# Two passes in place of three in the up projection of a transformer block, with the halves of a PSUM bank summed at eviction

## The reference

```python
h = rms_norm_2(x, g_pre_ffn) * (1.0 + sc2) + sh2          # 256 x 2048
u = causal_dwconv(h @ w_up, conv_w, conv_b)               # w_up 2048 x 11264, 3 taps over time
y = (silu(u[..., :D_FF]) * u[..., D_FF:]) @ w_down        # D_FF = 5632
x = x + gt2 * rms_norm_2(y, g_post_ffn)

def causal_dwconv(u, w, b):                               # per channel
    y = b
    for j in range(3): y = y + w[j] * up[:, j:j + S]      # up: u padded with 2 zero rows ahead
```

## Time and profile before

| | |
|---|---|
| runs | 2039.69, 2040.11 and 2041.86 us; median 2040.11 us |
| profiled execution | span 2036.7 us from its first to its last instruction; no other time of it is given |
| TensorE | busy 1953.7 us, 96% of the span |
| VectorE, ScalarE | busy 1321.1 us (65%) and 1018.2 us (50%) |
| DMA | 444.82 MB, mean 218 GB/s |
| mean granted TensorE clock | 0.984 |
| up projection | about 1263 to 1774 us of the span; down projection 1781 to 2021 us |

### The profile page before, as it was taken

One profiled execution on the slowest core, in us unless ns is written; L12 is line 12 of the kernel. 1 busy time (PEld: TensorE's weight loads), 2 busy tenths in 40 slices (PEclk: granted clock), 3 DMA queues, 4 the chain that ended last, 5 costly groups with the idle time before them and its releaser, 6 DMA issues.

```text
span 2036.7 us, 33083 instructions
## 1 busy us (share of the span) xinstructions
PE 1953.7 (96%) x11146; PEld 1695.5 (83%) x11146; DVE 1321.1 (65%) x1733; ACT 1018.2 (50%) x1587; POOL 112.6 (6%) x184
## 2 busy tenths in 40 slices
PE   6999999999999999998899998999999999999997
PEld 5888887778788887787778777999999999888885
DVE  5677775675777645557767777666677665655455
ACT  5544545553455454446654444555555555544443
POOL 1000001000000013320000000000000000000001
PEclk9999999998999999999999998999999999999998
DMA  7787786676787763346568885676767765555553
GB/s 255 258 299 251 251 270 198 207 263 238 259 293 256 275 181 115 113 131 219 177 211 280 297 264 177 204 231 225 234 221 230 231 200 183 165 176 192 198 187 124
DMA packets 236153, 444.82 MB, mean 218 GB/s; under 512 B 14125, under 2 KB 109962, under 8 KB 234682
## 3 DMA queue, kind: packets, MB, share of 16 engines
q1 hardware_dynamic: 234666, 434.39, 64.8%
q0 software_dynamic: 1424, 9.63, 1.2%
HBM read 439.72 MB, written 4.24 MB: 218 GB/s over the span
## 4 chain that ended last, share of the span: by engine, by line
PE 83%; DVE 6%; ACT 4%; issue 3%; DMA 3%; SPq 1%; DVEq 0%; ACTq 0%
PE PS L1575 74%; DMA ada_raw<-in_w_ada 3%; ACT w_hi L623 1%; PE PS L1606 1%; PE PS L1657 1%; DVE arena L1050 1%; DVE w_lo L1000 1%; PE PS L1634 1%; PE PS L1660 1%; PE PS L1643 1%; PE PS L1668 1%; DVE s_sb L1158 1%; DVE smx L1166 0%; PE PS L1678 0%; PE PS L1679 0%
## 5 line engine op out<-in xcount | busy, mean ns | idle before, releaser
L1000 DVE TENSOR_TENSOR w_lo<-raw,w_hi 128x1024 fp32r<-128x1024 f32 x618 | 755.7, 1224 | 556.4 <-ACT w_hi L623 549.0
L623 ACT ACTIVATE w_hi<-raw 128x1024 fp32r<-128x1024 f32 x618 | 653.1, 1059 | 734.7 <-PE PS L1575 689.9
L1575 PE MATMUL PS<-w_hi,aT_hi 128*128 128x512 f32 (+1 forms) x1632 | 651.9, 399 | 17.9 <-ACT arena L759 7.3
L1575 PE MATMUL PS<-w_hi,aT_lo 128*128 128x512 f32 (+1 forms) x1632 | 635.9, 390 | 0.0
L1575 PE MATMUL PS<-w_lo,aT_hi 128*128 128x512 f32 (+1 forms) x1632 | 635.1, 389 | 0.0
L1575 PE MATMUL PS<-aT_hi,w_hi 128*128 128x256 f32 x1408 | 398.9, 283 | 0.5 <-DVE aT_lo L1121 0.5
L1575 PE MATMUL PS<-aT_hi,w_lo 128*128 128x256 f32 x1408 | 398.4, 283 | 0.0
L1575 PE MATMUL PS<-aT_lo,w_hi 128*128 128x256 f32 x1408 | 398.4, 283 | 0.0
L1575 PEld LDWEIGHTS PS<-w_hi,aT_hi 128*128 128x128 f32 x1632 | 307.9, 189 | 95.6 <-issue 16.0
L1575 PEld LDWEIGHTS PS<-w_hi,aT_lo 128*128 128x128 f32 x1632 | 307.5, 188 | 64.6
L1575 PEld LDWEIGHTS PS<-w_lo,aT_hi 128*128 128x128 f32 x1632 | 308.2, 189 | 58.8 <-issue 0.2
(11 more groups left out here) (211 smaller groups left out, 1381.9 us busy)
## 6 DMA issues: line engine op xcount, KB each, us to landing
raw<-in_w_in SPq DMA_DIRECT2D x256, 512.0 KB, 4.0
ada_raw<-in_w_ada SPq DMA_DIRECT2D x192, 512.0 KB, 4.9
raw<-in_w_up SPq DMA_DIRECT2D x176, 512.0 KB, 3.5
raw<-in_w_down SPq DMA_DIRECT2D x88, 512.0 KB, 3.9
raw<-in_w_out SPq DMA_DIRECT2D x32, 512.0 KB, 4.8
raw<-in_w_o SPq DMA_DIRECT2D x32, 512.0 KB, 5.6
raw<-in_w_uq SPq DMA_DIRECT2D x18, 512.0 KB, 5.6
raw<-in_w_ukv SPq DMA_DIRECT2D x16, 512.0 KB, 4.0
```

Source lines behind the costliest of these rows:

```text
L623: nc.scalar.activation(w_hi[:, m % RING, :], raw[:, m % RING, :], ACT.Copy).then_inc(hi_ready, 1)
L1000: nc.vector.tensor_tensor(w_lo[:, m % RING, :], raw[:, m % RING, :], w_hi[:, m % RING, :].bitcast(F32), ALU.subtract).then_inc(lo_ready, 1)
L1575: mm = pe.matmul(dst, l, r, start=first and j == 0, stop=last and j == 2)
```

## The change

Activations: `aT_hi` and `aT_lo` become the two halves of one tensor `aT` [128, 16, 2, 256], so that for each k tile [a_hi | a_lo] are 512 contiguous columns. In the up projection a triple of passes becomes two: w_hi over the 512 columns [a_hi | a_lo] into a whole bank, and w_lo over a_hi (256 columns) into its first half. The bank then holds u in two parts. For each of the two tiles of a pair ScalarE copies the second half to SBUF (`cross`, in slots 0 and 1, semaphore `conv_b`), VectorE adds the first half to it in place (`sums`, in slots 1 and 2, semaphore `conv_sum`), and all taps read this sum from SBUF. The buffers of the sums (`halves`) lie in `bias`, which is not otherwise used in this phase. ScalarE's taps move to slots 2 and 3 and its silus to 4 and 5; VectorE's taps move to 3 and 4, its products to 5 and 6, its second GT2 piece to slot 7. The banks are handed back to TensorE by `conv_sum` in place of `conv_d`.

```diff
-        aT_hi = sb("aT_hi", [P, KT, SEQ], F32R)
-        aT_lo = sb("aT_lo", [P, KT, SEQ], F32R)
+        aT = sb("aT", [P, KT, 2, SEQ], F32R)
+        aT_hi, aT_lo = aT[:, :, 0, :], aT[:, :, 1, :]
+        halves = [[bias[:, 2 * SEQ * b + SEQ * k:2 * SEQ * b + SEQ * (k + 1)] for k in range(2)] for b in range(2)]
 # ScalarE, columns_hi (VectorE's columns_lo in the same way)
-                    last = nc.scalar.activation(dst[:, 2 * j:2 * j + 2, :].rearrange("p k t -> p (k t)"), bank,
+                    last = nc.scalar.activation(dst[:, 2 * j:2 * j + 2, :], bank.rearrange("p (k t) -> p k t", k=2),
 # ScalarE, up projection
-            def taps(pair, b, bank):
+            def cross(b, bank):
                 if b == 0:
                     act.wait_ge(chunk_used, T.ready(chunk_used, SLOTS))
+                for k in range(2):
+                    last = nc.scalar.activation(halves[b][k], PS[:, bank + 2 * k, SEQ:2 * SEQ], ACT.Copy)
+                last.then_inc(conv_b, 1)
+
+            def taps(pair, b):
+                act.wait_ge(conv_sum, T.ready(conv_sum))
                 act.wait_ge(y_done, T.free(y_done))
                 for k, (dst, tile) in enumerate(((conv_g[b], pair), (conv_u[b], pair + FT))):
-                    last = nc.scalar.activation(dst, PS[:, bank + 2 * k, 0:SEQ], ACT.Identity,
+                    last = nc.scalar.activation(dst, halves[b][k], ACT.Identity,
...
                 for slot in range(SLOTS):
                     split()
+                    if slot in (2, 3):
+                        taps(before + slot - 2, slot - 2)
                     if slot < 2:
-                        taps(before + slot, slot, (0 if odd else B_UP1) + slot)
-                    if slot in (3, 4):
-                        silu(slot - 3)
+                        cross(slot, (0 if odd else B_UP1) + slot)
+                    if slot in (4, 5):
+                        silu(slot - 4)
...
             up_panel(40, True)
             for b in range(2):
-                taps(42 + b, b, B_UP1 + b)
+                cross(b, B_UP1 + b)
+            for b in range(2):
+                taps(42 + b, b)
 # VectorE, up projection
+            def sums(b, bank):
+                dve.wait_ge(conv_b, T.ready(conv_b))
+                for k in range(2):
+                    last = nc.vector.tensor_tensor(halves[b][k], PS[:, bank + 2 * k, 0:SEQ], halves[b][k], ALU.add)
+                last.then_inc(conv_sum, 1)
+
-            def taps(pair, b, bank):
+            def taps(pair, b):
...
-                            out=dst[:, shift:SEQ], in0=PS[:, bank + 2 * k, 0:SEQ - shift],
+                            out=dst[:, shift:SEQ], in0=halves[b][k][:, 0:SEQ - shift],
...
                     if slot in (1, 2):
-                        taps(before + (slot - 1), slot - 1, (0 if odd else B_UP1) + slot - 1)
-                    if slot in (4, 5):
-                        product(before + (slot - 4), slot - 4)
-                    if slot in (0, 6) and kt is not None:
-                        ada(ADA_GT2, slot // 6, kt)
+                        sums(slot - 1, (0 if odd else B_UP1) + slot - 1)
+                    if slot in (3, 4):
+                        taps(before + (slot - 3), slot - 3)
+                    if slot in (5, 6):
+                        product(before + (slot - 5), slot - 5)
+                    if slot in (0, 7) and kt is not None:
+                        ada(ADA_GT2, slot // 7, kt)
 # TensorE, up_chunk
                     if slot == 0:
-                        pe.wait_ge(conv_d, T.free(conv_d))
+                        pe.wait_ge(conv_sum, T.free(conv_sum))
+                    bank = (B_UP1 if odd else 0) + 2 * (slot % 2) + e
+                    cols = slice(P * e, P * (e + 1))
                     for k in range(4):
                         kt = 4 * (slot // 2) + k
-                        mm = three(PS[:, (B_UP1 if odd else 0) + 2 * (slot % 2) + e, 0:SEQ], aT_hi[:, kt, :], aT_lo[:, kt, :],
-                                   wh[:, k, P * e:P * (e + 1)], wl[:, k, P * e:P * (e + 1)],
-                                   kt == 0, kt == KT - 1, weights_first=True)
+                        pe.matmul(PS[:, bank, :], wh[:, k, cols], aT[:, kt, :, :], start=kt == 0, stop=False)
+                        mm = pe.matmul(PS[:, bank, 0:SEQ], wl[:, k, cols], aT[:, kt, 0, :], start=False,
+                                       stop=kt == KT - 1)
```

More of the change, by code:

```diff
@@ L125, in block_kernel @@
                    "p_transposed": 1, "pT_full": 1, "o_ready": 1, "o_done": 1,
-                   "bias_used": 2, "gates_used": 1, "conv_d": 4, "y_done": 2,
+                   "bias_used": 2, "gates_used": 1, "conv_sum": 4, "y_done": 2,
                    "sb_w_done": 2, "sb_o_ready": 1, "sb_o_done": 1, "sb_transposed": 1, "sb_qkT": 1,
@@ L259, in block_kernel @@
         spread_done, g_read, g_copied = sem("spread_done"), sem("g_read"), sem("g_copied")
+        conv_b, conv_sum = sem("conv_b"), sem("conv_sum")
         conv_a, conv_d, conv_s, y_done = sem("conv_a"), sem("conv_d"), sem("conv_s"), sem("y_done")
@@ L949, in up_panel @@
                     split()
+                    if slot in (2, 3):
+                        taps(before + slot - 2, slot - 2)
                     if slot < 2:
-                        taps(before + slot, slot, (0 if odd else B_UP1) + slot)
-                    if slot in (3, 4):
-                        silu(slot - 3)
+                        cross(slot, (0 if odd else B_UP1) + slot)
+                    if slot in (4, 5):
+                        silu(slot - 4)
             first_panel(aT_hi, lambda k: gains[:, 1, k:k + 1], lambda k: mod[:, SH2, k:k + 1], banks=B_UP1)
             with T.loop(10, **{k: 4 * v for k, v in LANDED.items()}, free_chunk_used=16,
-                        ready_chunk_used=16, free_y_done=4, ready_conv_d=4) as i:
+                        ready_chunk_used=16, ready_conv_sum=4, free_y_done=4, ready_conv_d=4) as i:
                 up_panel(i * 4, True)
@@ L1006, in link @@
                 dve.wait_ge(dve_step, T.ready(dve_step))
-            give(dve, "acc_free0", "acc_free1", "ada_done", "s_read", "o_done", "bias_used", "conv_d", "y_done", "gates_used",
+            give(dve, "acc_free0", "acc_free1", "ada_done", "s_read", "o_done", "bias_used", "conv_sum", "y_done", "gates_used",
                  "sb_o_done")
@@ L1120, in columns_lo @@
                     bank = full
-                nc.vector.tensor_tensor(dst[:, 2 * j:2 * j + 2, :].rearrange("p k t -> p (k t)"), bank,
-                                        hi[:, 2 * j:2 * j + 2, :].rearrange("p k t -> p (k t)").bitcast(F32),
-                                        ALU.subtract).then_inc(aT_ready, 1)
+                nc.vector.tensor_tensor(dst[:, 2 * j:2 * j + 2, :], bank.rearrange("p (k t) -> p k t", k=2),
+                                        hi[:, 2 * j:2 * j + 2, :].bitcast(F32), ALU.subtract).then_inc(aT_ready, 1)
                 T.skip(aT_ready)
@@ L1513, in _ @@
             dve.wait_ge(ffn_row_landed, 32)
-            UP = dict(ready_hi_ready=16, ready_conv_a=4, ready_dve_step=4, ready_conv_s=4)
+            UP = dict(ready_hi_ready=16, ready_conv_b=4, ready_conv_a=4, ready_dve_step=4, ready_conv_s=4)
             with T.loop(8, **UP, ready_ada_landed0=32, ready_ada_landed1=32, ready_ada_done=4) as i:
@@ L1522, in _ @@
             for b in range(2):
-                taps(42 + b, b, B_UP1 + b)
+                sums(b, B_UP1 + b)
+            for b in range(2):
+                taps(42 + b, b)
             for b in range(2):
@@ L1566, in _, with three @@
                  "sb_zdone", "sb_cum", "sb_o_ready")
-            def three(dst, a_hi, a_lo, w_h, w_l, first, last, weights_first=False):
-                if weights_first:
-                    passes = ((w_h, a_hi), (w_h, a_lo), (w_l, a_hi))
-                else:
-                    passes = ((a_hi, w_h), (a_hi, w_l), (a_lo, w_h))
+            def three(dst, a_hi, a_lo, w_h, w_l, first, last):
+                passes = ((a_hi, w_h), (a_hi, w_l), (a_lo, w_h))
                 for j, (l, r) in enumerate(passes):
@@ L1880, in _ @@
                         lambda slot: 2 * (slot // 2) + 2)
-            with T.loop(10, ready_lo_ready=16, free_conv_d=4) as i:
+            with T.loop(10, ready_lo_ready=16, free_conv_sum=4) as i:
                 for odd in (True, False):
@@ L1887, in _ @@
             pe.wait_ge(ada_done, credits["ada_done"] + 64 + 96 + 32)
-            pe.wait_ge(conv_d, credits["conv_d"] + FT - 2)
+            pe.wait_ge(conv_sum, credits["conv_sum"] + FT - 2)
             spread(ADA_GT2, 0, range(4))
@@ L1897, in down @@
                     if first and s == 1:
-                        pe.wait_ge(conv_d, credits["conv_d"] + FT)
+                        pe.wait_ge(conv_sum, credits["conv_sum"] + FT)
                     for half in range(2):
```

## The result

Five executions of the changed kernel took 2020.86, 2021.94, 2023.38, 2033.96 and 2034.69 us; five of the kernel before 2039.69 to 2043.07, median 2041.86. But the five are not one group. Three lie within 2.5 us of each other, beside the forecast of 2022.2, and two are 11 to 14 us longer. By the ratio, 0.9935 x 2041.86 = 2028.6 us, the kernel is just outside the range that I gave (2019.6 to 2027.9), although its median alone lies inside it.

What follows compares the result with a forecast made beforehand. TensorE was taken as the bound: in the up projection, number of passes times the step between starts. 18.8 us gained less 0.9 at the end gives 17.9 off, span 2018.8 plus 3.4 around it, 2022.2 us; range 2019.6 to 2027.9.

Steps and rivals of the forecast that it cites:

- The passes: Up projection: each of 1408 triples goes from 360.0 to 346.7 ns as one wide and one narrow pass.
- the worst that I had worked out from the rows: Up projection: wide step of 230.7 ns from the latent projection, so a pair of 350.7 ns and a gain of 13.1 us.
- The gain of the passes: Up projection: 1408 passes saved at 13.33 ns each, 18.8 us off.
- The fixed part of 13.3 ns a pass: TensorE: price of a pass with its own weight load, whatever its width, left over from narrow and wide steps.
- The added work in the panels: Steady up projection panels: sums, copies and moved steps cost zero, hidden with about 6.0 us of lateness allowed.
- The end of the phase: After the last panel: copies and sums uncovered, VectorE's second taps become the bound, 0.9 us more, between 0 and 2.0.
- The low clock level: First down projection passes at the lower clock: 1.7 us lost, kept as is, anywhere from 0 to twice that.
- Layout and its writers: Activation writers of whole pairs get two runs of 256 columns: zero to 1 us, taken as zero.
- What lies around the span: Outside the traced span: the 3.4 us between span and median before, taken as the same for the changed kernel.

Runs made afterwards that it cites:

- e1: The changed kernel run again with no edit: 2020.63 to 2036.24 us, ratio 0.9924 to the kernel before.
- e2: The kernel before with only the new activation layout and its writers: median 2041.11 us, ratio 1.0005.
- e3: The changed kernel with three narrow passes kept in place of wide and narrow; copies, sums and moved steps included: median 2040.57 us, ratio 1.0000.
- e4: The kernel before with new layout and wide pass, no copies or sums, w_hi x a_lo left out of the result: 2020.37 to 2031.52 us, ratio 0.9924.
- e8: The changed kernel with a_hi and a_lo 16 KB apart, a second batch of e5's kernel: 2020.81 to 2022.68 us, ratio 0.9909.
- e13: The changed kernel unaltered once more, on the chip of e12: 2020.35 to 2033.47 us, ratio 0.9937.
- e17: The changed kernel with narrow before wide, GT2 spread and copy moved into the last panel, two y splits ahead of the last taps: median 2018.85 us, ratio 0.9886.
- e12: The changed kernel with a_hi and a_lo 16 KB apart, a third batch: 2021.46 to 2037.33 us, ratio 0.9942.
- e6: The changed kernel with four wide passes, then four narrow ones, per bank and chunk: median 2026.73 us, ratio 0.9932.
- e7: The changed kernel with passes ordered wide, narrow, narrow, wide, wide, narrow, narrow, wide: median 2024.04 us, ratio 0.9921.
- e5: The changed kernel with a_hi and a_lo 16 KB apart, first batch: 2022.56 to 2025.07 us, ratio 0.9920.
- e10: The changed kernel with GT2 spread and copy moved into the last panel and two y splits ahead of the last taps: 2017.79 to 2032.78 us, ratio 0.9910.
- e9: The changed kernel with halves 16 KB apart and the new end of the phase of e10: 2018.08 to 2021.08 us, ratio 0.9894.
- e18: The kernel of e17 again for more executions: median 2018.63 us, ratio 0.9890.

## Why the prediction was wrong, and where it was right

**The step that failed** is in "The passes": "I take 346.7, since both steps come from long unbroken streams". The value is right, but I took it as the one value of a pair. The stream of alternating widths has more than one steady pace, and which one it takes differs between executions of one kernel. In the traced long one a pair takes 353.1 ns, which is also above the worst that I had worked out from the rows (350.7). The gain is then 1408 x (360.0 - 353.1) = 9.7 us and not 18.8. The longest executions (2036 to 2037 us) would need about 357 ns a pair; none of those was traced. The two long executions of the result itself have no trace; if they took a second pace as e1's did, which is inferred, they and nothing else put the ratio outside the range. The rows could not show it: the kernel before has streams of one width only, and these do not vary (119.9 ns in its trace and those of e2 and e3). I had noted that the alternation is not in the trace, and bounded its mean by rows of other streams, but not its spread over executions. Some 22% of executions with wide before narrow being long by about 11 us puts 2 to 3 us on the mean, and more on a set of five with two long ones.

**The gain of the passes** in a quick execution: 346.3 ns a pair against 346.7. The fixed part of 13.3 ns a pass, and not the 2.5 ns of the Trainium skill ("TensorE: Matmul & The Clock Gate", section "Wait — 56ns, not 53.3ns?"), sized it; e4, the passes alone, shows the whole gain. By that figure of the Trainium skill 3.5 us would have been gained, an estimate; the traces do not agree with it.

**The added work in the panels** at nothing: right (e3: 119.9 ns a pass with all of it). The copies are cheaper than I took them, 371 ns and not 554 (in the groups of instructions of the changed kernel), the sums 417.

**The end of the phase**: 0.9 us forecast, 0.63 measured, by the mechanism forecast; the copies are what was mis-sized. The low clock level cost the same as before in the two traces, 238.50 and 238.35 us for the 1044 passes, and that was partly luck: with the same idle time as in the changed kernel they took 239.4 us in e1, e8 and e13 and 239.7 in e3. Against the 237.3 us of e17, with no fall of the clock, that is 1.1 to 2.5 us, within the zero to twice 1.7 that the prediction allowed.

**Layout and its writers** at nothing: right (e2: 1.0005).

**What lies around the span**: I took the 3.4 us between the span and the median of the kernel before as a fixed amount. It is 1.7 us in every execution whose span and time are both known (2021.94 and 2020.2; 2030.59 and 2028.9). The traced execution of before was then probably one of about 2038.4 us. Since both terms of the sum moved together, this did no harm to the forecast.

**What stays open.** Shown is that a long execution needs nothing but the alternating passes and their layout (e4), that it comes with the halves contiguous and 16 KB apart (e13, e12), that in the one traced no engine, load or granted clock is behind it (e1), and that other orders settle at other paces (e6, e7). Not shown is what in TensorE or its memory reads makes the second pace, why the padded kernel has none, how much of the share of long executions belongs to the chip, and whether narrow before wide avoids the slow pace or was lucky 17 times.

## What to carry to other kernels

In a stream in which TensorE is the bound and each pass loads its own weights, the number of passes counts beside the columns: here 13.3 ns a pass, the same for 256 columns and for 512, so two passes with the same stationary operand are worth joining wherever a bank has room, even at the price of a copy and a sum on engines with slack. Take a mixed stream's pace from several executions, not from one trace, and put variants that are to be compared on one chip. When work hides under TensorE in a loop, look at the last iteration by itself: there the same chain is in the open, and moving two small steps ahead of it took 1.8 us off TensorE's idle time.

## What the hardware did that was not expected

- One instruction stream, two steady paces at the same granted clock of 1.00: 346.3 and 353.1 ns a pair, each kept for the whole projection (the slow one seen in one trace); 11 long executions in 50, none in 80 of the kernel before.
- 32 bytes of padding in each half of the activation tensor made passes with it as stationary operand 5 to 6 ns longer (20.71 to 21.20 us for 90 passes), those with it as moving operand 1.8 ns, and cost 20 us in all; 16 KB between the halves cost nothing. I did not try other paddings. That the start of the rows at odd multiples of 32 bytes is what matters is a guess.
- Grouping equal widths was slower than alternating them: 350.4 ns a pair in the traced execution, the longest of five, against 346.3; by the medians, 3.1 us in all against e5 on the same chip.
- After the same 2.28 us of idle time the granted clock fell to 0.60 in e10 (0.58 in e9) and stayed at 1.00 in e17 and e18.
- A plain copy of 128 x 256 from PSUM on ScalarE took 371 ns where the scaled copy with bias of the same shape took 554.
